# The first pair's rope ahead of the decay-sum operations, and the decay sums ahead of a value projection

## The reference

```
z = h @ w_in                       # queries, keys, values of 12 dilated and 4 forgetting heads, + 4 gates
o_dil = dilated_attention(rope(q), rope(k), v)          # three causal windows, merged
logf  = log_sigmoid(zf + b_forget);  c = cumsum(logf)   # per forgetting head
o_fox = softmax(q k^T / 8 + c_i - c_j, causal) @ v
y = [rms(o_dil)*g_dil, rms(o_fox)*g_fox] @ w_out
h = LN(alpha*h + y)
h = LN(alpha*h + MoE(h))           # 16 experts of 3 matrices 1024 x 1024, two experts per token
```

## Time and profile before

| what | value |
|---|---|
| median of three runs | 1317.68 us |
| the profiled execution's own time | 1319.99 us |
| its span, first to last instruction | 1318.3 us |
| TensorE matmuls busy | 1102.9 us, 84% of the span |
| VectorE busy | 351.1 us, 27% |
| ScalarE busy | 184.8 us, 14% |
| mean granted clock of TensorE | 0.913 |
| chain that ended last | PE 54%, DMA 38%, issue 4%, DVE 3% |
| attention stage of layer 0, first pair's projections to first expert load | about 23 to 57 us |
| HBM traffic | 443 MB read, mean 337 GB/s |

### The profile page before, as it was taken

How to read it: one execution, slowest core, us unless ns; L and a number is a source line. 1 busy time by engine, 2 the same in 40 slices (tenths; PEclk the granted TensorE clock), 3 DMA queues, 4 the chain that set the end, 5 groups by cost and what they waited for, 6 DMA issues and landing times.

```text
span 1318.3 us, 17515 instructions
## 1 busy us (share of the span) xinstructions
PE 1102.9 (84%) x6296; PEld 555.2 (42%) x6297; DVE 351.1 (27%) x853; ACT 184.8 (14%) x375; POOL 4.6 (0%) x12
## 2 busy tenths in 40 slices
PE   7999988799976769777899997898998976766685
PEld 5667553344432323323667653344343332322232
DVE  0665560111111111112176463112011111111123
ACT  2223210000010000010223330101001000010000
POOL 0000000000000000000000000000000000000000
PEclk9899998899988889879889998899999987887888
DMA  9814389999999999999931433268999999999994
GB/s 376 341 56 175 132 354 427 383 429 430 430 429 428 427 428 428 430 400 424 390 128 64 181 136 164 94 289 350 429 366 397 428 429 429 429 428 429 428 402 180
DMA packets 34712, 444.71 MB, mean 337 GB/s; under 512 B 4080, under 2 KB 4336, under 8 KB 5872
## 3 DMA queue, kind: packets, MB, share of 16 engines
q1 hardware_dynamic: 33520, 439.97, 80.0%
q0 software_dynamic: 1152, 4.19, 0.8%
HBM read 443.11 MB, written 1.05 MB: 337 GB/s over the span
## 4 chain that ended last, share of the span: by engine, by line
PE 54%; DMA 38%; issue 4%; DVE 3%; ACT 0%; DVEq 0%; ACTq 0%; SPq 0%
DMA ring<-in_w_down_dram 38%; PE lo L580 12%; PE acc L491 9%; PE lo L592 8%; PE acc L469 5%; PE lo L567 4%; PE lo L687 3%; PE acc L555 3%; PE acc L645 2%; PE lo L555 1%; PE acc L533 1%; PE lo L521 1%; PE lo L508 1%; PE lo L510 1%; PE acc L754 1%
## 5 line engine op out<-in xcount | busy, mean ns | idle before, releaser
L592 PE MATMUL lo<-ring,work 128*32 128x512 f32 x2304 | 300.0, 668 | 144.6 <-DMA ring<-in_w_down_dram 128.4
L592 PEld LDWEIGHTS lo<-ring,work 128*32 128x32 f32 x2304 | 78.3, 118 | 341.3 <-issue 174.8
L580 PE MATMUL lo<-ring,work 128*64 128x512 f32 x864 | 196.6, 611 | 26.9 <-issue 21.4
L567 PEld LDWEIGHTS lo<-work,h 128*128 128x128 f32 x1152 | 138.3, 193 | 65.0 <-issue 60.0
L567 PE MATMUL lo<-work,h 128*128 128x128 f32 x1152 | 156.8, 285 | 3.0 <-DVE work L1310 1.9
L580 PEld LDWEIGHTS lo<-ring,work 128*64 128x64 f32 x864 | 63.4, 141 | 152.7 <-issue 146.1
L491 PE MATMUL acc<-ring 128*128 128x256 f32 x512 | 124.0, 399 | 0.0
L491 PEld LDWEIGHTS acc<-ring 128*128 128x128 f32 x512 | 101.5, 201 | 21.0 <-issue 7.0
L1026 ACT ACTIVATE work<-lo 64x512 f32<-64x512 f32 x24 | 14.3, 594 | 486.9 <-PE lo L592 486.9
L1389 DVE COPY work<-lo 128x512 f32<-128x512 f32 x24 | 16.6, 692 | 237.6 <-PE lo L592 237.6
L469 PE MATMUL acc<-ring 128*128 128x512 f32 x128 | 62.7, 635 | 3.9 <-ACT ring L924 3.9
(11 more groups left out here) (190 smaller groups left out, 661.0 us busy)
## 6 DMA issues: line engine op xcount, KB each, us to landing
ring<-in_w_gate_dram SPq DMA_DIRECT2D x64, 2048.0 KB, 17.9
ring<-in_w_up_dram SPq DMA_DIRECT2D x64, 2048.0 KB, 24.3
ring<-in_w_down_dram SPq DMA_DIRECT2D x64, 2048.0 KB, 23.8
ring<-in_w_in_dram SPq DMA_DIRECT2D x24, 1024.0 KB, 25.8
ring<-in_w_out_dram SPq DMA_DIRECT2D x8, 1024.0 KB, 28.4
ln_gb<-in_ln_dram POOLq DMA_DIRECT2D x8, 512.0 KB, 11.6
cst<-in_consts_dram SPq DMA_DIRECT2D x1, 1420.0 KB, 17.7
h<-in_x_dram SPq DMA_DIRECT2D x1, 1024.0 KB, 5.4
```

What stands on the lines that cost most here:

```text
L567: mm = nc.tensor.matmul(lo[:, 2 + k // 4, (k % 4) * P:(k % 4 + 1) * P], h[:, t, k * P:(k + 1) * P], place_t[:, t], start=(k % 4 == 0 and t ...
L580: mm = nc.tensor.matmul(lo[half * W:(half + 1) * W, bank, :], lhsT, ring[:, s, at:at + 512], start=start, stop=stop, skip_group_check=True)
L592: return nc.tensor.matmul(lo[at * T:(at + 1) * T, bank, :], lhsT, ring[:, s, col:col + 512], start=start, stop=stop, skip_group_check=True)
```

## The change

On TensorE the call of `sum_decay` in the loop's first turn, with its wait for the constants, moves ahead of the value projection, right behind the first pair's projections. On VectorE the first pair's rope moves from the loop's first turn to the place right behind `fold_norm`, ahead of the wait for `cum_done` and of the four operations that follow it. No instruction is added or taken away, and sizes are the same.

```
@@ TensorE
                     queries_keys(l, p, second_half, fulls)
+                    if p == 0:
+                        pe.wait_ge(const_full, 16 * CONST_LOADS)
+                        sum_decay(l)
                     if p >= 2:
                         weigh_values(l, p - 2, ring_free[QK_SLOT[p]])
                     if p < 6:
                         release = {0: ring_free[QK_SLOT[0]], 1: ring_free[QK_SLOT[1]]}.get(p)
                         values(l, 1 + p // 2, (first_half, second_half)[p % 2], fulls, release)
-                    if p == 0:
-                        pe.wait_ge(const_full, 16 * CONST_LOADS)
-                        sum_decay(l)
@@ VectorE
                 fold_norm(l)
+                rope(l, 0)
                 v.wait_ge(cum_done, l + 1)
                 take_totals()
@@ VectorE, loop over the pairs
-                    if p < PAIRS_DIL:
+                    if 1 <= p < PAIRS_DIL:
                         rope(l, p)
```

## The result

The changed kernel takes 1302.82 us (median of four runs, 1301.46 to 1304.05) against 1317.92 us before: ratio 0.9881 with a 95% interval of 0.987 to 0.9893. The forecast was 1306.2 us, with a range from 1304.0. Twelve more runs of the same kernel came later; the mean of all sixteen is 1304.2 us (1300.83 to 1306.64), that of 68 runs of before 1318.3 us (1313.39 to 1321.81). That is 14.0 us, and the spread of single runs is wider than the first four of each showed.

What follows compares the result with a forecast made beforehand. The bound was taken to change by stage, with TensorE bounding the touched attention stage. Gains of 4.7 (wait), 6.8 (clock) and 0 (swap) made 11.5 us: 1317.68 to 1306.2 us, own range 1304 to 1308, 8-in-10 range 1304.0 to 1312.5.

Steps and rivals of the forecast that it cites:

- The wait: TensorE's 2.34 us wait for the first pair's rope at the scores goes in both layers: 4.7 us.
- The swap at nothing: Decay sums ahead of the value projection on TensorE: put at 0, ends -0.2 and +0.4 us per layer.
- The clock: Second pair's bias spreading and projections stay at full clock instead of half: 3.4 us per layer, 6.8 in all.
- rival 1: Clock falls again briefly behind scores and spreading, 1.7 us per layer: 1307.9 (one layer) or 1309.6 us (both); chance 0.30.
- The tight place: VectorE's second rope ends at 52.9 us, TensorE asks at 53.8: hidden with 0.9 us to spare.
- The shift reaches the end: Expert stage's saturated weight transfers start from TensorE's progress and move with it, so the whole 11.5 us carries through.
- the low end of the range: Whole kernel: 1304 us, from the duration rows, the swap's gain and one half-speed stretch less elsewhere.
- the 0.6 us that the duration rows add: Second pair's projections and spreading: duration rows give 7.4 us for both layers, against 6.8 by the clock.

Runs made afterwards that it cites:

- rope only: Against the kernel before, only VectorE's move of the first pair's rope, with TensorE's old order: 1305.65 us, ratio 0.9903.
- filling the wait alone: The kernel before with five overwritten matmuls per layer put into TensorE's wait ahead of the first scores: 1311.23 us, ratio 0.9946.
- the thirteen matmuls: The changed kernel with thirteen overwritten full-speed matmuls per layer on TensorE ahead of the first scores: 1317.89 us, ratio 1.0.
- its halves: Against the kernel before, only the rope moved (1305.65 us), and only the decay sums moved (1308.48 us).
- the two kernels with spread gates: Rope only with the forget gates' matmuls spread among the first pair's projections, starting behind the first or third matmul: 1306.05 and 1305.72 us.
- before's second trace: The kernel before run again unchanged, with a second trace: 1317.99 us, ratio 1.0004.
- the changed kernel's second: The changed kernel run again unchanged, with a second trace: 1305.14 us, ratio 0.9903 to before.
- eight added matmuls: The changed kernel with eight overwritten full-speed matmuls per layer on TensorE ahead of the first scores: 1312.55 us, ratio 0.9951.

## Why the prediction was right or wrong

- **The wait.** Right. 2.34 us per layer are gone, the rope runs from 31.98 to 36.19 (forecast 32.75 to 36.96, TensorE being 0.8 us earlier before it), and line 1224 ends with 3.1 us to spare (forecast 3.0).
- **The swap at nothing.** Right for its place behind the early rope: rope only and the full change can't be told apart, and from the first pair's projections to the first scores both take 17.39 us. What I missed is that the swap by itself removes the wait too; I computed it only together with the rope's move.
- **The clock.** Right in size and cause: 3.65 and 1.92 us against the forecast's 3.46 and 1.73, and filling the wait alone brought 7.1 us where 6.8 were put down. But I treated the fall as a yes or no of the kernel. It is in part one of the execution: of the three traces of the changed kernel one has a half-speed stretch there in one layer, as rival 1 had it. The two attention parts fell by 11.3 us in the means of the traces, and the sum said 11.5.
- **The tight place.** The second rope started at 47.62 and ended at 51.83, TensorE asked at 53.20: 1.4 us to spare, forecast 0.9.
- **The shift reaches the end.** Right, by the thirteen matmuls that take it all back. The third pair's projections are ahead by 6.5 us in layer 0 (49.65 against 56.15) and 14.1 in layer 1 (663.62 against 677.73), where 5.7 and 11.5 were forecast: 0.8 was there ahead of the first pair, and the rest of layer 0 gave 2.1 more.
- **The step that failed** is the low end of the range: "down by the 0.6 us that the duration rows add, by the swap's gain and by one half-speed stretch less elsewhere". By the prediction's own numbers that is 0.6 + 0.4 (the swap's 0.2 in each layer) + 1.7 = 2.7 us, so 1303.5, put down as 1304.0. The only allowance for the rest of the kernel, some 1210 of its 1318 us, was one half-speed stretch of 1.7 us; that the rest might repeat itself less well was put at nothing. The runs show in its place: the 68 runs of before spread over 8.4 us, where the three at hand had 0.9; one choice of the clock at one item is worth 2.7 us, the whole allowance; and between the traces of the changed kernel the rest of layer 0 differs by 2.2 us (576.85 to 579.04) and that of layer 1 by 3.4 (625.42 to 628.86). In the pair of traces of the first comparison the two rests gave 3.9 us and the attention parts 11.8. That the median of the first four lies below the range is partly luck: the mean of all sixteen, 1304.2, is just inside it.
- **What stays open.** Chance explains why four runs gave 15.1 us, but not quite why sixteen give 14.0 and not 11.5. The second item of layer 1 takes 1.8 us of the 3.5 by which the means of the last column differ. Some 1.7 us are left there: 628.6 (so corrected) for the changed kernel and 628.7 for its halves against 630.3 for before. A steady effect of arriving earlier would fit these, and thirteen added matmuls (630.2), but not the two kernels with spread gates, which arrive as early and have 629.8 and 630.5. Each is one trace, and no run here settles it.

## What to carry to other kernels

Where the engine that sets the end waits for another, look behind the wait as well: here 2.3 us of idle time in front of small matmuls cost another 3.4 in granted clock, and even 1.1 us of it cost 1.7. When a chain is late, compute each edit alone before putting two together; here either was enough. And take the allowance for the rest of the kernel from many runs or from two traces of the same kernel, not from the agreement of three runs.

## What the runs showed of the hardware that was not expected

A wait of TensorE can be kept from lowering the clock by useless matmuls: 2.2 us of them in a 2.34 us wait left the clock at 1.00 behind it. Behind a block of 32 four-column matmuls without any idle time the 32 matmuls of the first pair's projections took 8.84 us, with a half-speed stretch, in 21 of the 24 layers that have the block, and 7.15 us, at full speed, in three: layer 0 of before's second trace, of the changed kernel's second and of the thirteen matmuls. In the second of these it was the scores and the spreading behind which the clock fell instead. The same matmuls mixed with 256-column ones did not lower it in either layer of the two traces. An idle time in the expert stage was followed by half speed in eleven traces and by full speed in three, and its length did not decide it: 3.31 us (eight added matmuls) was followed by half speed, 3.77 us (the changed kernel's second trace) by full speed.
